# Output projections cut by query columns, residual additions ahead of their low parts, and one norm moved

## The reference

```
for l in range(2):
    u = rmsnorm(h, norm_gain[l]) @ w_in[l]          # queries, keys, values, gates
    do = diff_attention(...)  -> subln, * silu(dg)   # 4 heads of 128
    fo = forgetting_attention(...) * silu(fg)        # 8 heads of 64
    h = h + concatenate([do, fo]) @ w_out[l]         # the output projection
```

```
x = x + softmax(q k^T / 8) v @ mem_wo                # memory attention, 4 heads of 64
x = x + 0.5 * (silu(n @ wg) * (n @ wu)) @ wd         # n = rms_norm(x), 2816 hidden
```

## Time and profile before

| | |
|---|---|
| median of 3 runs | 1998.16 us (1996.62 to 2007.05) |
| profiled execution | 1999.93 us, span 1998.1 us |
| mean granted TensorE clock | 0.989 of full speed |
| TensorE matmul, busy | 1924.0 us (96%), 10942 instructions |
| TensorE weight load, busy | 1643.1 us (82%), 10942 |
| VectorE / ScalarE / GpSimd, busy | 755.9 / 707.1 / 712.7 us (38 / 35 / 36%) |
| DMA | 144.22 MB, mean 72 GB/s |

### The profile page before, as it was taken

One profiled execution on the slowest core, in us unless ns is written; L12 is line 12 of the kernel. 1 busy time (PEld: TensorE's weight loads), 2 busy tenths in 40 slices (PEclk: granted clock), 3 DMA queues, 4 the chain that ended last, 5 costly groups with the idle time before them and its releaser, 6 DMA issues.

```text
span 1998.1 us, 26646 instructions
## 1 busy us (share of the span) xinstructions
PE 1924.0 (96%) x10942; PEld 1643.1 (82%) x10942; DVE 755.9 (38%) x1288; ACT 707.1 (35%) x1328; POOL 712.7 (36%) x342
## 2 busy tenths in 40 slices
PE   7999989999998999999999999899999989999999
PEld 7999878989987887888888877789767768888887
DVE  6422373454125526441112255546676441111001
ACT  3112355321125545223222223335564542222211
POOL 4333201253332114555554423320003325555443
PEclk9999899999999999999999999899999989999999
DMA  4222200122221002233322233210003212222323
GB/s 142 84 76 84 64 1 1 53 85 85 75 79 48 1 11 89 96 95 95 95 90 93 94 111 117 65 43 1 1 1 112 79 53 94 92 93 93 99 87 108
DMA packets 40585, 144.22 MB, mean 72 GB/s; under 512 B 4624, under 2 KB 4880, under 8 KB 40336
## 3 DMA queue, kind: packets, MB, share of 16 engines
q1 hardware_dynamic: 40464, 142.51, 22.2%
HBM read 140.40 MB, written 2.10 MB: 71 GB/s over the span
## 4 chain that ended last, share of the span: by engine, by line
PE 86%; DVE 7%; ACT 3%; issue 1%; DMA 1%; POOL 1%; SPq 0%; DVEq 0%; ACTq 0%
PE ps L353 22%; PE ps L354 22%; PE ps L355 22%; PE ps L820 5%; PE ps L801 5%; PE ps L810 3%; DMA raw<-wstream 1%; PE ps L1965 1%; PE ps L1948 1%; PE ps L937 1%; PE ps L480 1%; POOL wl L349 1%; ACT wh L341 1%; PE ps L1937 1%; DVE xl L409 1%
## 5 line engine op out<-in xcount | busy, mean ns | idle before, releaser
L349 POOL TENSOR_TENSOR wl<-raw,wh 128x1024 fp32r<-128x1024 f32 (+2 forms) x254 | 604.5, 2380 | 863.7 <-ACT wh L341 863.7
L353 PE MATMUL ps<-xh,wh 128*128 128x512 f32 (+1 forms) x1728 | 622.4, 360 | 26.2 <-POOL wl L349 13.6
L354 PE MATMUL ps<-xl,wh 128*128 128x512 f32 (+1 forms) x1728 | 615.7, 356 | 0.0
L341 ACT ACTIVATE wh<-raw 128x1024 fp32r<-128x1024 f32 (+2 forms) x254 | 266.0, 1047 | 983.9 <-PE ps L355 914.0
L355 PE MATMUL ps<-xh,wl 128*128 128x512 f32 (+1 forms) x1728 | 613.9, 355 | 0.0
L353 PEld LDWEIGHTS ps<-xh,wh 128*128 128x128 f32 x1728 | 327.4, 189 | 82.4 <-issue 20.5
L354 PEld LDWEIGHTS ps<-xl,wh 128*128 128x128 f32 x1728 | 327.7, 190 | 49.8 <-issue 1.9
L355 PEld LDWEIGHTS ps<-xh,wl 128*128 128x128 f32 x1728 | 327.8, 190 | 48.3
L1064 POOL TENSOR_TENSOR xl<-xb,xh 128x512 fp32r<-128x512 f32 (+1 forms) x22 | 26.1, 1185 | 329.2 <-ACT xh L973 329.2
L354 PE MATMUL ps<-aL,wh 128*128 128x512 f32 x352 | 139.3, 396 | 0.0
L355 PE MATMUL ps<-aH,wl 128*128 128x512 f32 x352 | 139.1, 395 | 0.0
(11 more groups left out here) (331 smaller groups left out, 2551.1 us busy)
## 6 DMA issues: line engine op xcount, KB each, us to landing
raw<-wstream SPq DMA_DIRECT2D x236, 512.0 KB, 3.5
raw<-wstream SPq DMA_DIRECT2D x16, 384.0 KB, 3.0
raw<-wstream SPq DMA_DIRECT2D x10, 528.0 KB, 3.5
h<-xT SPq DMA_DIRECT2D x4, 528.0 KB, 6.0
out<-h SPq DMA_DIRECT2D x8, 256.0 KB, 3.4
hm<-memT SPq DMA_DIRECT2D x1, 1024.0 KB, 4.8
cst<-const SPq DMA_DIRECT2D x1, 720.5 KB, 8.9
cst<-const SPq DMA_DIRECT2D x1, 320.0 KB, 4.0
```

What stands on the lines that cost most here:

```text
L341: e.activation(wh[p % 2][:, 0:n], raw[c % 2][:, 0:n], ACT.Copy).then_inc(*w_hi(p))
L349: e.tensor_tensor(wl[p % 2][:, 0:n], raw[c % 2][:, 0:n], wh[p % 2][:, 0:n].bitcast(F32), ALU.subtract).then_inc(*w_lo(p))
L353: e.matmul(o, w_h, x_h, start=start, stop=False)
L354: e.matmul(o, w_h, x_l, start=False, stop=False)
```

## The change

Both output projections of the first block: tiles 0 and 1 are made in pieces of columns, for all eight k (`part_of_tile`, new). In layer 0 the early pieces are the 264 columns of half 0 and the first 136 of half 1, and the late piece the last 128; in layer 1 they are columns 0 to 191, 192 to 383 and, late, 384 to 511. The early pieces wait for the third query tile's group only, the late ones for the fourth. The order on TensorE is: early pieces of tile 0, with the held-back transposes of the last group behind the first of them; early pieces of tile 1; late piece of tile 0; late piece of tile 1; then tiles 2 to 7 as before. Memory attention's projection has the same for tiles 0 to 2 with 384 columns early and 128 late. In its residual additions VectorE adds tile m and then makes the low part of tile m-1. In ffn2 the norm's matmuls move from behind g0 to behind u0.

```
@@ -373,6 +373,21 @@
                             k == 0, k == nk - 1)
             if last:
                 r.then_inc(*tile(*key))
+            return r
+
+        def part_of_tile(e, on, key, o, half, lo, hi, x, c0, src):
+
+            p = PART[key]
+            hh, ll = wh[p % 2], wl[p % 2]
+            th, tl = src
+            on.wait_ge(*w_hi[p])
+            on.wait_ge(*w_lo[p])
+            a, b = c0 + o.shape[2] * half + lo, c0 + o.shape[2] * half + hi
+            for k in range(KT):
+                for s in x(k):
+                    on.wait_ge(*s)
+                r = mm3(e, o[:, half, lo:hi], hh[:, 128 * k:128 * k + 128], ll[:, 128 * k:128 * k + 128],
+                        th[:, k, a:b], tl[:, k, a:b], k == 0, k == KT - 1)
             return r
 
         def normed(st):
@@ -764,6 +779,9 @@
                                 self.ends.setdefault(u + x.job + 1 + k, []).append((x.group, k))
                 self.steps = 1 + max(self.ends)
 
+                group = units[-1].group
+                self.held = (group, 1) if group[0] in ("fox", "mem") else None
+
             def copied(self, u):
                 return (v_flip if self.on_dve[u] else a_flip)[self.name, u]
 
@@ -821,7 +839,8 @@
                                      x.value(j, b - a), start=j == 0, stop=j == len(x.blocks) - 1)
                     r.then_inc(*pv(name, u))
                 for key, k in plan.ends.get(s, []):
-                    end_pe(e, on, plan, key, k)
+                    if (key, k) != plan.held:
+                        end_pe(e, on, plan, key, k)
 
         def attention_act(e, on, plan):
             units, name = plan.units, plan.name
@@ -1200,13 +1219,29 @@
                 feature_tile(e, on, key, out_of(key, n), n, c0, x, src)
                 yield c
 
-        def layer_ao(l):
-            return lambda k: [s["ao", "diff" if k < 4 else "fox", l, 3] for s in (x_hi, x_lo)]
+        def layer_ao(l, i=3):
+            return lambda k: [s["ao", "diff", l, 3] if k < 4 else s["ao", "fox", l, i] for s in (x_hi, x_lo)]
 
         def wout_pe(e, on, l):
             n, c0 = shape(l, "out")
-            for _ in residual_pe(e, on, ("wout", l), layer_ao(l), n, c0, pair, X[l]):
-                pass
+
+            early = [(0, 0, 192), (0, 192, 384)] if l else [(0, 0, 264), (1, 0, 136)]
+            late = (0, 384, 512) if l else (1, 136, 264)
+            for c in range(2):
+                claim(on, pair(("wout", l, c)), 2 if n > 512 else 1, v_out["wout", l, c])
+            for c in range(2):
+                key = ("wout", l, c)
+                for i, part in enumerate(early):
+                    part_of_tile(e, on, key, out_of(key, n), *part, layer_ao(l, 2), c0, X[l])
+                    if c == 0 and i == 0:
+                        end_pe(e, on, plans[l], *plans[l].held)
+            for c in range(2):
+                key = ("wout", l, c)
+                part_of_tile(e, on, key, out_of(key, n), *late, layer_ao(l), c0, X[l]).then_inc(*tile(*key))
+            for c in range(2, KT):
+                key = ("wout", l, c)
+                claim(on, pair(key), 2 if n > 512 else 1, v_out[key])
+                feature_tile(e, on, key, out_of(key, n), n, c0, layer_ao(l), X[l])
 
         def next_of(l, c):
 
@@ -1285,11 +1320,10 @@
                 ps = claim(on, pair((st, f)), 2, v_out[st, "gated", f])
                 for s, part in enumerate(("g", "u")):
                     feature_tile(e, on, (st + part, f), three(ps, 2)[:, s:s + 1, :], T, M, normed(st))
-                    if f == 0 and s == 0:
-                        if st == "ffn1":
-                            final_pe(e, on)
-                        else:
-                            norm_pe(e, on, st, T, 1, pair(st), SUMMED(st))
+                    if f == 0 and s == 0 and st == "ffn1":
+                        final_pe(e, on)
+                    if f == 0 and s == 1 and st == "ffn2":
+                        norm_pe(e, on, st, T, 1, pair(st), SUMMED(st))
             for m in range(KT):
                 ps = claim(on, pair((st, "d", m)), 1, v_out[st, "half", m])
                 for q, (f0, nf) in enumerate(((0, 8), (8, 8), (16, 6))):
@@ -2064,14 +2098,29 @@
                     turned_scale_pe(e, on, "memkv", [0, 128], rstm, SINGLES)
                     head_norm_pe(e, on, ("mq", 1), SINGLES)
             attention_pe(e, on, plans["mem"])
-            for half in range(2):
-                for mi in range(4):
-                    m = 4 * half + mi
-                    claim(on, pair(("mo", m), SINGLES), 1, v_out["mo", m])
-                    r = feature_tile(e, on, ("mo", half), out_of(("mo", m), T), T, 0,
-                                     lambda k: [s["ao", "mem", 3] for s in (x_hi, x_lo)], (amh, aml), nk=2, col=mi, last=mi == 3)
-                    if mi < 3:
-                        r.then_inc(*rows("mo", m))
+
+            def mo_cols(m, a, b, group):
+                p, w = PART["mo", m // 4], 128 * (m % 4)
+                hh, ll = wh[p % 2], wl[p % 2]
+                on.wait_ge(*w_hi[p])
+                on.wait_ge(*w_lo[p])
+                on.wait_ge(*x_hi["ao", "mem", group])
+                on.wait_ge(*x_lo["ao", "mem", group])
+                o = PS[:, 512 * bank["mo", m] + a:512 * bank["mo", m] + b]
+                for k in range(2):
+                    r = mm3(e, o, hh[:, 512 * k + w:512 * k + w + 128], ll[:, 512 * k + w:512 * k + w + 128],
+                            amh[:, k, a:b], aml[:, k, a:b], k == 0, k == 1)
+                return r
+            for m in range(3):
+                claim(on, pair(("mo", m), SINGLES), 1, v_out["mo", m])
+                mo_cols(m, 0, 384, 2)
+                if m == 0:
+                    end_pe(e, on, plans["mem"], *plans["mem"].held)
+            for m in range(3):
+                mo_cols(m, 384, T, 3).then_inc(*rows("mo", m))
+            for m in range(3, KT):
+                claim(on, pair(("mo", m), SINGLES), 1, v_out["mo", m])
+                mo_cols(m, 0, T, 3).then_inc(*(rows("mo", m) if m % 4 < 3 else tile("mo", m // 4)))
 
         def mo_done(m):
             return rows["mo", m] if m % 4 < 3 else tile["mo", m // 4]
@@ -2155,11 +2204,14 @@
                     r = e.tensor_copy(QM[64 * j:64 * j + 64, 2 * c + j, :], src[64 * j:64 * j + 64, :])
                 r.then_inc(*v_out("mq", c, "put"))
             attention_dve(e, on, plans["mem"])
-            for m in range(KT):
-                on.wait_ge(*mo_done(m))
-                e.tensor_tensor(h[:, m, M:L], h[:, m, M:L], PS[:, 512 * bank["mo", m]:512 * bank["mo", m] + T],
-                                ALU.add).then_inc(*v_out("mo", m))
-                gained_lo(e, on, "ffn2", m, h[:, m, M:L], P_("g_ffn2", m, m + 1), xh[:, m, M:L], xl[:, m, M:L])
+            for m in range(KT + 1):
+                if m < KT:
+                    on.wait_ge(*mo_done(m))
+                    e.tensor_tensor(h[:, m, M:L], h[:, m, M:L], PS[:, 512 * bank["mo", m]:512 * bank["mo", m] + T],
+                                    ALU.add).then_inc(*v_out("mo", m))
+                if m:
+                    gained_lo(e, on, "ffn2", m - 1, h[:, m - 1, M:L], P_("g_ffn2", m - 1, m), xh[:, m - 1, M:L],
+                              xl[:, m - 1, M:L])
             for m in range(KT):
                 add_square(e, on, "ffn2", m, T)
```

## The result

| | before | after |
|---|---|---|
| median of 22 runs each, us | 1999.41 (1996.62 to 2009.45) | 2004.34 (2000.71 to 2010.57) |
| ratio, 95% interval | | 1.0022 (1.0013 to 1.0031) |
| span of the profiled execution, us | 1998.1 | 1998.9 |
| TensorE matmuls | 10942 | 11104 |

The change makes the kernel slower by 0.22%, which is 4.4 us (the medians themselves lie 4.9 us apart): less than the half per cent that the prediction counts as no change, but clear of zero. The two profiled spans differ by 0.8 us only, so the seams have to be measured one by one, each from the start of its last value products (the row of 20 matmuls, in seam C the row of 8). These are TensorE's rows of the changed kernel that answer to the earlier trace rows: start, duration, what, count, idle before and releaser.

The account below looks back on a forecast made before the run. TensorE, 86% of the last-ending chain, was taken as the bound, so only its waits and low-clock stretches could yield time. Terms 2.9 + 2.7 + 1.5 - 1.9 gave +5.2 us: 2003 us against the median, range 1994 to 2010.

Parts of the forecast that it names:

- seam C: Memory attention, its projection and the start of ffn2: 1.9 us won.
- the clock fall: One fall of TensorE's clock counted for the two layers' attention-to-projection stretches: 1.5 us lost, bounds 0 and 4.
- Price of a piece: Projection matmuls: every piece up to 192 columns takes 0.107 us, the time of a weight load.
- the bounds from the slope: Lower bounds from time per column, 0.45 ns: 0.058 us for 128 columns, 0.088 for 192.
- Seam A: Layer 0's attention into its output projection: 18.0 us against 15.06, a loss of 2.9 us.
- seam B: Layer 1's attention into its output projection: 17.2 us against 14.48, a loss of 2.7 us.
- Wait before tile 2: Both layers' projections: TensorE stalls 1.4 us for tile 2's weights, whose buffers tile 0 now frees late.
- First ffn2 tile 8.0 us sooner: Start of ffn2 after memory attention: first tile at 1612.1 instead of 1620.14, bounds 1610 and 1613.5.
- Wait before g1, 5.4 us: In ffn2 behind the moved norm: TensorE stands 5.4 us because ScalarE splits g1's weights only after Ln and Exp.
- Two cold starts at 2.05: ffn2 tiles g0 and g1 each start at the lower clock after a gap: 2.05 us each, 4.1 us together.
- The rival in which weight-bound streams lose the clock: Pieces in the layers' projections run at the low clock, their loads taking twice as long: 2028 us, chance 0.12.
- The rival of the free norm: In ffn2 the norm's move costs nothing, g1 starts at 1625, 7 us won: 1998 us, chance 0.06.

Follow-up runs that it names:

- The experiment with 384 columns: Changed kernel with one wide early piece of 384 columns in layer 1 instead of two of 192; ratio to the kernel before 1.0018.
- the layers alone: Kernel before with only the two layers' projections cut into pieces, memory attention, additions and norm as before; ratio to the kernel before 1.0043.
- the norm back: Changed kernel with the norm's matmuls put back behind g0; ratio to the kernel before 1.0001.
- splits first: Changed kernel with ScalarE's splits of the weights of g1 and u1 ahead of the norm's Ln and Exp; ratio to the kernel before 0.9992.
- tile 0 sooner: Changed kernel with tile 0's late piece ahead of tile 1's early ones in both layers; ratio to the kernel before 1.0013.
- halves: Changed kernel with both layers' tiles 0 and 1 in two pieces only, 264 columns (layer 0) and 256 (layer 1); ratio to the kernel before 0.9965.
- halves and splits: Changed kernel with two half-tile pieces in both layers and ScalarE's weight splits ahead of the norm; ratio to the kernel before 0.9946.
- other banks: Halves and splits, plus one pair of PSUM banks skipped ahead of ffn2; ratio to the kernel before 0.9920, median 1983.08 us.
- the last kernel of the series: Other banks, but with the layers' projections in whole tiles as in the kernel before; ratio to the kernel before 0.9952.

## Why the prediction was right

It gave +5.2 us on the profiled execution, no change within 0.5%; the ratio gave +4.4, the medians +4.9, the seams +4.0. The mechanism was right in all its parts but one, the clock fall, and part of the closeness is luck: the 1.5 us that didn't come was partly made good by pieces that cost more than foreseen, and the whole kernel's gap happened to come out nearer to 5.2 than the seams' sum, within an interval of 2.6 to 6.2 us. By its own steps:

- **Price of a piece**: 0.107 us foreseen, 0.112 measured; the bounds from the slope (0.058, 0.088) were wrong. The Trainium skill gives 81 ns for load-and-matmul pairs of 128 columns ("TensorE: Matmul & The Clock Gate", section "Back-to-back issue gap"). These traces don't agree: 112 ns. The experiment with 384 columns shows that it isn't something else in the seam. That a weight load is what takes the 0.11 us stays inferred: 128, 136 and 192 columns have the same spacing, 256 and more do not. The records of the weight loads don't settle it, for they last 0.19 us each and overlap, beside 192 columns as beside 384.
- **Seam A** +2.9 foreseen, +3.2 measured; **seam B** +2.7 foreseen, +3.3 (against an execution whose clock fell there; against one without, 4.6). The 5 ns more per piece make 0.5 and 0.7 us with 96 and 144 of them, the shorter wait before tile 2 takes 0.3 back in each, and some 0.2 us in each stay unexplained.
- **Wait before tile 2**: 1.4 us foreseen, 1.06 and 1.08 measured, gone when tile 0 is released sooner.
- **A clock fall in A or B, +1.5**: it did not come. This is the term that failed. Around tile 2's start the granted clock was 1.00 in both layers of the changed kernel and of seven experiments with pieces in the layers (the layers alone, the norm back, splits first, tile 0 sooner, halves, halves and splits, other banks); only with the piece of 384 columns did it fall, in layer 1 (mean 0.83 from 748 to 758). That is one fall in the 18 seams of nine profiles.
- **First ffn2 tile 8.0 us sooner**: 8.28. **Wait before g1, 5.4 us**: 4.82. **Two cold starts at 2.05**: both came; g0's 24 matmuls took 1622.41 - 1615.18 = 7.23 us instead of 5.6, 1.6 more, and g1's 1642.56 - 1634.70 = 7.86 us, 2.26 more. **Seam C -1.9**: -2.5.
- **The rival in which weight-bound streams lose the clock** did not show in the seams, but what the runs show of the clock (below) is close to it. **The rival of the free norm** priced itself too low: it had seam C win 7 us, and where ScalarE's splits come first the tail is 402.3 - 392.55 = 9.8 us shorter than before.

## What to carry to other kernels

Cutting a matmul's columns to fill a wait is free only while a matmul of half the columns takes half the time: here pieces of 256 columns were nearly free (about 0.12 us, half of the 0.2335 of 512), while those of 128 and 192 both cost 0.11, and 240 small pieces cost more than the waits they removed in the layers. An output tile that frees a shared buffer must not finish late just because the wait inside it is gone; look at who refills the buffer. Before moving an instruction behind another, read every queue for what stands behind its consumer: the norm's move by one tile held up the weights of the tile after.

## What the runs showed of the hardware

About the same stretch of sparse attention, from the same code, ran at either clock for a long time. First the changed kernel, then the kernel with the wide piece, 20 us each, in the columns of the earlier trace rows:

```profile
1340.00:1360.00 20.00, 18.12 (x155) 17.30 (x155) 12.85 (x41) 11.62 (x47) 1.26 (x1) 1.00 0.00 1
```

```profile
1340.00:1360.00 20.00, 20.00 (x99) 19.82 (x99) 6.65 (x22) 8.01 (x34) 0.00 (x0) 0.50 0.00 1
```

155 matmuls against 99. In the second the low level lasted from about 1335.6 to 1365.9, although TensorE was busy throughout; the last kernel of the series had a stretch of some 30 us at the same place (0.50 from 1328 to 1356). Elsewhere the low level was left sooner: in the projections with 512 columns within 3 to 6 us of their first matmul in the profiles of before and after, and after some 4 us also in an attention stretch of small matmuls (284 to 288 before, 128 and 144 columns, weight loads busy throughout). So a stretch of small matmuls doesn't always keep it, and what brings these long stretches was not tried.

The kernel with the wide piece took 2013.95 us in its profiled execution with a median of 2000.44, the last one 1997.01 with 1988.01, and the kernel before ranges up to 2009: such stretches would explain the spread, which the profiles of these two long executions suggest and don't prove.

A gap on TensorE was followed by a fall in some executions and by none in others. The 2.44 us wait before g0 was followed by one in the changed kernel (0.50 from 1616 to 1619), but in the kernel with the wide piece g0 kept the full clock behind the same wait, and its tail (398.2) is 1.6 us shorter for it. A forecast that prices a fall behind every gap has to allow for either outcome.
